# Two-layer backbone on one core: routing scratch moved into the attention output's area, expert 0's first product placed inside the routing, and the second pair of experts moved ahead of the third single one

## The reference

```
h  = norm1(ALPHA * x + gate * (attention @ w_out)) * (1 + scale) + shift
s  = sigmoid(h @ router)                       # 64 scores for each token
w, idx = top 8 of s + bias, in the best 4 of 8 groups;  w = w / sum(w) * 2.5
y  = sum over the 8 experts e of a token: w_e * (silu(h @ wg[e]) * (h @ wu[e])) @ wd[e]
x  = norm2(ALPHA * x + gate2 * (y + shared(h)))
```

## Time and profile before

| | us |
|---|---|
| three runs | 1833.87, 1835.21 (median), 1835.61 |
| profiled execution, its own time | 1842.93 |
| span of its instructions | 1841.5 |
| layer 0: routing begins, first block's product ends, last block's down product ends | 357, 389, 943 |
| layer 1: the same three | 1191, 1222, 1784 |
| PE busy, share of the span | 87% |
| DMA read and written over the span | 335 GB/s |

### The profile page before, as it was taken

The page is one execution under the profiler, slowest core; times in us unless marked ns, Lnnn a source line. Parts: engine busy times, 40 slices in busy tenths (PEclk is TensorE's granted clock), DMA queues, the critical chain, the costliest instruction groups (busy, mean ns, idle before and its releaser), DMA issues. The chain is left out here.

```text
span 1841.5 us, 19074 instructions
## 1 busy us (share of the span) xinstructions
PE 1596.3 (87%) x6864; PEld 766.5 (42%) x6864; DVE 584.1 (32%) x1348; ACT 353.5 (19%) x766; POOL 267.3 (15%) x233
## 2 busy tenths in 40 slices
PE   4998867999798898989877989999799898988867
PEld 1665523554243343433324854554343343333323
DVE  2233554633131111111118873643122111111107
ACT  2214511111111111111123154111111111111120
POOL 0000101112111122111102400011111122111101
PEclk8999897999899999999988989989899999999988
DMA  9880276479999999999977013578999999999956
GB/s 389 328 337 9 75 278 254 178 297 360 422 387 420 404 418 413 420 419 416 394 282 275 6 48 110 219 306 340 419 375 420 401 416 401 421 419 402 407 212 261
DMA packets 112001, 587.22 MB, mean 319 GB/s; under 512 B 22184, under 2 KB 24520, under 8 KB 54176
## 3 DMA queue, kind: packets, MB, share of 16 engines
q1 hardware_dynamic: 88480, 532.46, 71.5%
q0 software_dynamic: 22848, 50.47, 7.2%
q10 hardware_dynamic: 576, 3.03, 0.4%
HBM read 570.99 MB, written 46.35 MB: 335 GB/s over the span
## 5 line engine op out<-in xcount | busy, mean ns | idle before, releaser
L2784 DVE TENSOR_TENSOR scratch<-scratch,bank 128x256 f32<-128x256 f32 x84 | 51.5, 613 | 642.5 <-ACT scratch L2757 613.7
L2676 PE MATMUL bank<-scratch 128*64 128x512 f32 x384 | 191.1, 656 | 51.9 <-DMA weights<-in_moe_w_up 41.1
L2676 PE MATMUL bank<-weights,scratch 128*64 128x512 f32 x384 | 183.2, 634 | 40.5 <-DMA scratch<-in_moe_w_up 28.0
L2677 PE MATMUL bank<-scratch 128*64 128x512 f32 x416 | 196.6, 629 | 0.0
L2677 PE MATMUL bank<-weights,scratch 128*64 128x512 f32 x384 | 192.5, 660 | 0.0
L2757 ACT ACTIVATE scratch<-bank 128x256 f32<-128x256 f32 x84 | 32.2, 384 | 678.8 <-PE bank L2677 450.6
L2676 PEld LDWEIGHTS bank<-scratch 128*64 128x64 f32 x384 | 55.9, 151 | 177.7 <-issue 177.7
L2676 PEld LDWEIGHTS bank<-weights,scratch 128*64 128x64 f32 x384 | 54.1, 145 | 160.3 <-issue 160.3
L2430 POOL DMA_INDIRECT hP<-h_rows,tok_idx x78 | 81.9, 1050 | 161.6 <-PE bank L2391 65.9
L2445 POOL DMA_INDIRECT y_rows<-z,y_idx x38 | 39.6, 1043 | 452.6 <-ACT z L2765 366.3
L2445 POOL DMA_INDIRECT y_rows<-hP,y_idx x40 | 41.7, 1043 | 391.8 <-ACT hP L2765 305.2
(11 more groups left out here) (380 smaller groups left out, 2508.3 us busy)
## 6 DMA issues: line engine op xcount, KB each, us to landing
weights<-in_moe_w_gate SPq DMA_DIRECT2D x60, 1024.0 KB, 13.7
weights<-in_moe_w_up SPq DMA_DIRECT2D x60, 1024.0 KB, 21.9
weights<-in_moe_w_down SPq DMA_DIRECT2D x60, 1024.0 KB, 21.8
scratch<-in_moe_w_gate SPq DMA_DIRECT2D x58, 1024.0 KB, 13.3
scratch<-in_moe_w_up SPq DMA_DIRECT2D x58, 1024.0 KB, 22.3
scratch<-in_moe_w_down SPq DMA_DIRECT2D x58, 1024.0 KB, 21.1
weights<-in_w_mod SPq DMA_DIRECT2D x6, 2048.0 KB, 11.4
wmod_more<-in_w_mod SPq DMA_DIRECT2D x6, 2048.0 KB, 8.7
```

What stands on the lines that cost most here:

```text
L2676: nc.tensor.matmul(out[0:HALF, :], x[:, 0:HALF], w0[:, kk], start=(kk == 0), stop=(kk == KT - 1))
L2677: m = nc.tensor.matmul(out[HALF:P, :], x[:, HALF:P], w1[:, kk], start=(kk == 0), stop=(kk == KT - 1))
L2784: nc.vector.tensor_tensor(B.h[b % 2].rearrange("p (j q) -> p q j", j=2), B.ex[b % 2].rearrange("p (q j) -> p q j", j=2), k.ps[2 + b % 2][: ...
```

## The change

- The routing's scratch goes from `scratch` into `cat`, whose contents are used up by then. Slot 3's first load no longer waits for `s_end`.
- All three fixed experts are loaded in the projection stage. For this, `w_out`'s second half goes from `scratch[1024:5120]` to two pieces elsewhere (each half of `w_out` is loaded by two DMAs of 1 MB), and the norm's work row is the one row `M.tmp`, with a wait of DVE for its own last result.
- On PE the matmul for the sorted order (`sorted_id`) goes ahead of `maskT`; DVE copies it into `k.perm` at once, before it waits for the sorted counts.
- On PE `turn_first` goes ahead of the sorted counts, and block 0's gate-up product (`gate_up_first`) into the routing, ahead of the token lists. The wide matmuls without use (`pe_keep_warm(k, 3, 2)`) are gone.
- The lists of block groups 0 and 1 are both made within the routing (the second in a place of its own, `le_1`), and the gathers of the third and fourth block no longer wait for one of the experts' stage. The row numbers of both groups come behind block 1's product.
- `block_plan` takes j - 1 for j: the order is S0, S1, P14, P15, S2, P16, P17, S3, ... instead of S0, S1, P14, S2, P15, P16, S3, ..., and it ends ..., P36, P37, S13, P38 instead of ..., P36, S13, P37, P38. The shared blocks stay at 9, 18, 27.
- The fold's rows in layer 0 move from `cat` to `z`, and the copy of block 1's result waits for their store.

```diff
-FIXED_SEM = (2, 3, 0)
-EARLY_EXPERTS = 2
+FIXED_SEM = (2, 3, 5)
...
-def out_slots(k):
-    return early_slot(k), k.s[:, 1024:5120].rearrange("p (k n) -> p k n", k=KT)
+def out_halves(k, c):
+
+    if c == 0:
+        whole = early_slot(k)
+        return whole[:, 0:KT // 2], whole[:, KT // 2:KT]
+    return tuple(k.s[:, a:a + 2048].rearrange("p (k n) -> p k n", k=KT // 2) for a in (8960, 15104))
...
-            for e in range(EARLY_EXPERTS):
+            for e in range(FIXED):
                 load_fixed(k, sp, layer, e)
...
                 nc.vector.tensor_scalar(M.nb[:, t:t + 1], mu, rstd, -1.0, ALU.mult, ALU.mult).then_inc(s_nb, 1)
+                dve.wait_ge(s_h, t + 1)
...
-        for e in range(EARLY_EXPERTS, FIXED):
-            load_fixed(k, sp, layer, e)
         if folds:
             sp.wait_ge(s_fs, 5)
             F.store(sp, s_fd)
...
-        pool.wait_ge(s_tk, 1)
+        pool.wait_ge(s_tk, 2)
...
         m.then_inc(s_cnt, 1)
+        pe.wait_ge(s_pm, 1)
+        nc.tensor.matmul(sorted_id, k.c(C_COL + 1, 1, NE), Pm[0:NE, :], start=True, stop=True).then_inc(s_id, 1)
         for t in range(TILES):
             m = nc.tensor.matmul(maskT[:, t * P:(t + 1) * P], m3[:, t, :], k.ident, start=True, stop=True)
         m.then_inc(s_cnt, 1)
-        pe.wait_ge(s_pm, 1)
+        turn_first()
         pe.wait_ge(s_cb, 2)
...
-        pe.wait_ge(s_le, 1)
-        pe_count(k, L, 0, 1).then_inc(s_ix, 1)
-        pe.wait_ge(s_cb, 4)
-        pe_keep_warm(k, 3, 2)
-        turn_first()
+        gate_up_first()
+        for g in range(2):
+            pe.wait_ge(s_le, g + 1)
+            pe_count(k, L, g, 1).then_inc(s_ix, 1)
         pe.wait_ge(s_dt, 1)
...
+        dve.wait_ge(s_id, 1)
+        nc.vector.tensor_copy(k.perm[0:1, :], sorted_id).then_inc(s_perm, 1)
+        copy_first()
         dve.wait_ge(s_so, 1)
...
-        while (solo - 2) * (PAIRS - 1) < j * (SOLO - 2):
+        while (solo - 2) * (PAIRS - 1) < (j - 1) * (SOLO - 2):
...
                 if after[i] is not None:
                     sp.wait_ge(s_gu, after[i] + 1)
-                elif slot[i] == FIXED:
-                    sp.wait_ge(s_end, 1)
...
-        count(0)
         for b in range(N):
-            gate_up(b)
-            if b + 1 < len(COLUMNS):
-                count(b + 1)
+            if b:
+                gate_up(pe, b)
+            if 1 <= b < len(COLUMNS):
+                count(b)
...
-            rt_pe(pe, lambda: first[0](pe, 0))
+            rt_pe(pe, lambda: first[0](pe, 0), lambda: first[3](pe, 0))
```

More of the change, by code:

```diff
@@ L186, in __init__ @@
         self.s_const = ctx.enter_context(nc.semaphore("const_loaded"))
-        self.s_ahead = [ctx.enter_context(nc.semaphore(f"ahead{i}_loaded")) for i in range(5)]
-        self.ahead = [0] * 5
+        self.s_ahead = [ctx.enter_context(nc.semaphore(f"ahead{i}_loaded")) for i in range(6)]
+        self.ahead = [0] * 6
         self.s_late = [ctx.enter_context(nc.semaphore(f"late_half{i}_in")) for i in range(3)]
@@ L1872, in stage_project_norm @@
     M = NormBuffers(k, 1)
-    w_slot = out_slots(k)
+    w_half = [out_halves(k, c) for c in range(2)]
     cat = cat_turned(k)
@@ L2029, with lists @@
 COLUMNS = [(0, 4), (SOLO, 5), (4, 5), (SOLO + 5, 5), (9, SOLO - 9), (SOLO + 10, 5), (SOLO + 15, 5), (SOLO + 20, PAIRS - 20)]
+def lists(L, g):
+    return L.le_1 if g == 1 else L.le
 def columns_of(col):
@@ L2059, in pe_count @@
                 out, by = L.counts[:, r:r + m, :], k.count_by[:, t, r:r + m, :]
-            ins = k.nc.tensor.matmul(out, L.le[:, t, e * P:(e + 1) * P], by, start=(t == 0), stop=(t == TILES - 1))
+            ins = k.nc.tensor.matmul(out, lists(L, g)[:, t, e * P:(e + 1) * P], by, start=(t == 0), stop=(t == TILES - 1))
     return ins
@@ L2153, in route_programs @@
     Pm = cut(NE)
-    assert o <= 15104, o
+    assert o <= TILES * D, o
     logits = k.ps[7][:, 0:E3]
     total, totalT = k.ps[3][:, 0:NE], k.ps[5][0:NE, 0:P]
-    maskT, nthT, nth = k.ps[0][0:NE, 0:TOK], k.ps[1][0:NE, 0:TOK], k.ps[2][:, 0:E3]
+    maskT, nthT, nth = k.ps[5][0:NE, P:P + TOK], k.ps[3][0:NE, NE:NE + TOK], k.ps[4][:, 0:E3]
     steps, first_row = k.ps[4][:, 256:256 + E3], k.ps[4][:, 448:448 + NE]
@@ L2226, in on_tensor @@
             nc.tensor.matmul(tile3(sorted_incl)[:, t, :], IT[0:NE, t * P:(t + 1) * P], Pm[0:NE, :], start=True, stop=True)
[L2227 to L2228 removed]
+        nc.tensor.matmul(sorted_total, CB[0:NE, :], Pm[0:NE, :], start=True, stop=True).then_inc(s_so, 1)
         pe.wait_ge(s_cb, 3)
@@ L2556, in experts_programs @@
     rank_at = [r for _, _, ranks in plan for r in ranks]
-    fixed_at = [k.ahead[s] + (48 if e >= EARLY_EXPERTS else 0) for e, s in enumerate(FIXED_SEM)]
+    fixed_at = [k.ahead[s] for s in FIXED_SEM]
     shared_at = k.ahead[3] + 48
@@ new lines, in gate_up @@
+    def gate_up(pe, b):
+        tile, at, ranks = plan[b]
+        if ranks:
+            pe.wait_ge(s_xa, order[b] + 1)
+            pe.wait_ge(s_xv, order[b] + 1)
+            for i in range(at, at + len(ranks)):
+                if nth[i] is None:
+                    pe.wait_ge(k.s_ahead[FIXED_SEM[slot[i]]], fixed_at[slot[i]])
+                else:
+                    pe.wait_ge(s_wg[slot[i]], 32 * nth[i])
+        elif tile == 0:
+            pe.wait_ge(k.s_ahead[3], shared_at)
+        ge(pe, s_h, b - 1)
+        out = k.ps[2 + b % 2]
+        if len(ranks) == 2:
+            w0, w1 = (expert_views(k, slot[i])[3] for i in (at, at + 1))
+            for kk in range(KT):
+                x = B.xT[:, kk * P:(kk + 1) * P]
+                nc.tensor.matmul(out[0:HALF, :], x[:, 0:HALF], w0[:, kk], start=(kk == 0), stop=(kk == KT - 1))
+                m = nc.tensor.matmul(out[HALF:P, :], x[:, HALF:P], w1[:, kk], start=(kk == 0), stop=(kk == KT - 1))
+        else:
+            w = expert_views(k, slot[at])[3] if ranks else shared_views(k)[3]
+            for kk in range(KT):
+                x = B.xT[:, kk * P:(kk + 1) * P] if ranks else k.hT[:, kk, tile * P:(tile + 1) * P]
+                m = nc.tensor.matmul(out[:], x, w[:, kk], start=(kk == 0), stop=(kk == KT - 1))
+        m.then_inc(s_gu, 1)
@@ L2732, in finish_wait @@
         eng.wait_ge(s_d, b + 1)
+        if layer + 1 < DEPTH and order.get(b) == 1:
+            eng.wait_ge(s_fd, 32)
         if b in order:
```

99 lines of the change are left out of this document (39 added, 60 removed).

## The result

The changed kernel takes 1826.81 us (median of five runs, 1819.34 to 1834.00); the kernel before took 1835.61 in five runs beside them (1833.87 to 1837.50). The ratio is 0.9945, 95% interval 0.9918 to 0.9971: faster by 0.5%. The forecast was 1830.7, with 1821 to 1840 as its range.

What follows compares the result with a forecast made beforehand. The prediction took the stream of expert weights to bound the experts' stage; start -6.5, idle time -6.0 and tail +8.0 sum to -4.5 us, from 1835.21 to 1830.7, with a range of 1821 to 1840.

Steps and rivals of the forecast that it cites:

- Start of the stream: First expert load after the routing goes out earlier, 4.0 us in layer 1 and 2.5 in layer 0: -6.5 together.
- the ledger: Each layer's end is stream start, plus idle time in the stream, plus fixed bytes, plus PE's work behind the last bytes.
- Idle time: DMA gaps early in the experts' stage, 13.5 us in both layers, shrink: 9.0 gained at full clock, 3.0 at half; 6.0 taken.
- not in the sum: Later layer 1 stretch at DMA share 0.85, a like one in layer 0: possible 5 us more, kept for the low end.
- Block 0: Its gate-up product within the routing ends (G0) 5 to 7.5 us earlier; half clock would make it 3 later.
- PE's wait at the first turn: Sign that the forecast is wrong: PE waiting for the first gather where block 0's rows are turned.
- Tail: Each layer's end: P38 behind S13 waits for weights and takes 9.86 us, 4.0 later per layer, 8.0 lost together.
- Expert 2's load: Moved from the routing to the projection stage, where the DMA share is 0.10: nil; at most 7.7 us per layer if colliding.
- slot 3's wait: Slot 3's first load goes out 6.9 us behind the first, one expert takes 7.7: removing the wait gives next to nothing.
- Free tail: Rival, chance 0.18: the new order costs nothing at the layers' ends; -12.5 us, 1822.7.
- Gaps come back: Rival, chance 0.17: idle time at the stream's start is not filled; +1.5 us, 1836.7, no change.
- Late gather: Rival, chance 0.15: PE waits at block 0's turn for the first gather, 5 us per layer; +5.5 us, 1840.7, slower.

Runs made afterwards that it cites:

- e_perm_late: Changed kernel with the cast of the sorted order and its matmul's result place put back, so the first expert load goes out late: 1824.51 us, ratio 0.9942.
- e_old_order: Changed kernel with the old order of blocks throughout, early first block and early sorted order kept: 1822.54 us, ratio 0.9919.
- e_warm: Changed kernel plus two useless 512-column matmuls in layer 1 ahead of the first block's turn: 1828.01 us, ratio 0.9946.
- e_e2_late: Changed kernel with expert 2's three matrices loaded within the routing again, as in the kernel before: 1825.60 us, ratio 0.9945.
- e_tail_wait: Changed kernel with the old order in the list's second half and slot 3's first load again waiting for the routing's end: 1817.33 us, ratio 0.9894.
- e_first_late: Changed kernel with block 0's gate-up product moved behind the routing's last matmul: 1835.42 us, ratio 1.0000.
- e_two_parts: Changed kernel with old order in the second half; late sorted-order cast, expert 2's load in the routing and slot 3's wait put back: 1822.02 us, ratio 0.9917.

## Why the prediction was right, and where it was not

- **What bounds, and the sign.** Right: the weight stream bounds the stage, and the new order has its price at the end. The time lies 3.9 us below the forecast.
- **Start of the stream, -6.5.** Moved nearly as forecast in layer 0, by 2.2 (2.5), and by 5.5 in layer 1, where I had 4.0 (the table; in the other kernels with the early order it is 3.0 to 4.4). But the term does not exist: put back by 2.6 and 6.7 us, it cost nothing (`e_perm_late`). The step that failed is the ledger, which took start and idle time as two independent terms. What counts is when PE frees the slots. The shift of the start is given back as idle time, up to where the share is 1.00, which `e_perm_late` has reached; a still later start was not tried by itself.
- **Idle time, -6.0, and 5 us "not in the sum".** Mis-sized, and this carries the gain. By the ledger, L less the first load fell by 9.9 in layer 0 and 2.1 in layer 1, 12.0. By the runs' rule the terms are: block 2 earlier, 7.7 and 4.5; and L - G2 shorter, 4.4 and 3.0. Together 19.6, which is by construction what L came earlier (12.1 and 7.5), where I had 6.5 + 6.0 = 12.5. I left out the later stretch. Its share did go from 0.85 to 0.99, and `e_old_order` has 0.95 in the like stretch of layer 0. For leaving it out I had cited the Trainium skill, DMA: Bandwidth & Descriptors, Latency and other measured facts, that two of the 16 DMA engines are usually slower, so that the slowest would have no idle time to give. The mean share's gain was real here.
- **Block 0.** Forecast 5 to 7.5 earlier, measured 8.4 and 4.7. In layer 1's profile both of the things that I had set against it happened: PE reached the turn 2.1 us behind the gather's issue, not 3.7, and waited 1.35; and the clock was half. PE's wait at the first turn was one more of the prediction's signs of being wrong; it came true in layer 1 (in layer 0 the wait was 0.4). G0 at full clock is the usual case, 17.8 to 19.7 in the other kernels with this product in the routing. The rule that I cited (the Trainium skill, TensorE: Matmul & The Clock Gate, Part 1: lower clock when idle) agrees in kind with the 1.35 us, and also with the half clock at 1187 to 1191 in `e_warm`, where PE was busy but had stood idle 1.83 us up to 1184.67. It does not fit the fall at 373.3 in the kernel before, where PE was busy 3.09 of the 3.30 us ahead of it.
- **Tail, +8.0.** Right in mechanism and nearly in size: 4.4 and 4.9, so 9.3. P38 behind S13 waits 4.25 and takes 9.97 in layer 1 (forecast 9.86), and takes 8.75 in layer 0; P37 has almost no wait (0.93 in layer 1).
- **Expert 2's load, nil; slot 3's wait, nil.** The first is confirmed within what the runs can tell (`e_e2_late`). The second is not: I priced the wait as it stood in the kernel before, 6.9 us behind the first load against 7.7 for one expert. With block 0's product in the routing the same wait would last until 13 us behind it (1197.78 less 1184.82 in `e_tail_wait`), and the DMA then runs dry (share 0.27). Its removal belongs to the move of block 0, and I had it as a part by itself.
- **The rivals.** *Free tail* is refuted: the tail costs 9.3, and with the old one behind the kernel is 11.5 us faster. Its time of 1822.7 came near the measured one for another reason. *Gaps come back* is half true: what the earlier start gave did come back as gaps, the rest did not. *Late gather* happened in one layer at 1.35 us (0.4 in the other), not at 5.

That the forecast came close was luck in good part, because two errors met: 6.5 for a start worth nothing, and 6.0 where PE's earlier blocks and the better order gave 19.6.

By the medians, of the 8.8 us gained: block 0's product in the routing is worth 8.6 (`e_first_late`, which has the new order), and the order costs 4.3 (`e_old_order`). Each was taken out of the whole alone, so the two need not add up to 8.8; what the list of group 1 within the routing gives was not measured by itself. The order could have been a gain: the new order in front and the old one behind takes 1815.3, 20 us (1.1%) faster than the kernel before. It has the lowest time of all kernels measured here.

## What to carry to other kernels

Where a compute engine works without a gap while the DMA share is below 1, the transfers wait for buffers, and only that engine's next releases move the end; an earlier first load just lengthens the idle time. This holds while no load waits for something else: in `e_tail_wait` one that was held behind the routing's end moved the last landing by 4 us in layer 1 although PE was busy 64.10 of 65 us. Test it by moving the first load later: if the share rises to 1.00 and the end stays, the start was never the bound. An order of work has a good pattern in front (free buffers early) and another behind (little work after the last bytes, no wait ahead of the last product); choose them separately.

## What the hardware showed that I had not expected

- A half-speed stretch of the granted clock fell in or just ahead of the routing in every profiled layer, often with PE busy in it (0.57 over 4.00 of 4.00 us in `e_warm`), but in 27 of 28 layers one fell 0.2 to 3.5 us behind an idle wait of 1.8 us. With this product within the routing, G0 came at 20.9 where the low clock met it (layer 1 of the changed kernel), and at 17.8 to 19.7 where it lay over the small matmuls.
- Executions of one kernel differ by up to 15 us (1819 to 1834). The routing's first counting matmul alone varies by 9 us (354.1 to 363.5 in layer 0) between profiled executions of kernels that are the same up to there; compare stretches from a common instruction on, not from the span's start.
- The last landing follows the end of block 2's product, 520 us earlier, within 2 us in layer 0 (521.4 to 523.3 in the profiled executions of the twelve kernels with the new order in front, while G2 itself moved by 6). In layer 1 it is 527.8 to 530.3 in ten of them, and 531.0 and 533.0 in the two in which slot 3's first load waits for the end of a routing that has block 0's product in it (`e_two_parts`, `e_tail_wait`).
